# Key blocks of the first grouped attention in pairs on TensorE: two transposes, two gate pieces, two products

## What is computed

```python
def nsa_attention(...):            # 8 heads in 2 groups; per chunk of 128 queries
    sc = q @ kc * scale                       # 31 compressed keys
    ss = q @ k_slc * scale + bias             # selected keys (causal here)
    sw = q @ k_win * scale + bias             # window of 512 keys
    return gs[0] * softmax(sc) @ vc + gs[1] * softmax(ss) @ v_slc + gs[2] * softmax(sw) @ v_win
def swa_sink_attention(...):       # 8 heads, 2 kv heads, window of 128 keys, a sink in the softmax
    ...
y = sigmoid(gate_a) * (o_a @ w_up_nsa) + sigmoid(gate_b) * (o_b @ w_up_swa)
```

## Time and profile before

| | us |
|---|---|
| median of 3 runs | 1619.71 (1619.16 to 1621.48) |
| profiled execution | 1620.14 |
| its span in the trace | 1618.3 |
| the first grouped attention in it | about 130 to 332 |

### The profile page before, as it was taken

One profiled execution on the slowest core, in us unless ns is written; L12 is line 12 of the kernel. 1 busy time (PEld: TensorE's weight loads), 2 busy tenths in 40 slices (PEclk: granted clock), 3 DMA queues, 4 the chain that ended last, 5 costly groups with the idle time before them and its releaser, 6 DMA issues.

```text
span 1618.3 us, 23738 instructions
## 1 busy us (share of the span) xinstructions
PE 1553.6 (96%) x8400; PEld 1220.1 (75%) x8400; DVE 1002.4 (62%) x2286; ACT 757.2 (47%) x1426; POOL 504.8 (31%) x231
## 2 busy tenths in 40 slices
PE   7998999999899999999999999999999989999998
PEld 5886666678688888888887787778777768866666
DVE  6235546355679867655788756676677267147854
ACT  6225676634343323233444554445545443247753
POOL 3651232245244444444321212211114453320012
PEclk9999999999999999999999999999999989999998
DMA  6861112274356565653210111111101122220001
GB/s 200 174 165 34 60 59 67 72 271 131 104 175 202 184 201 189 197 152 92 79 53 27 40 40 39 40 51 33 44 26 57 49 67 91 66 67 13 1 23 57
DMA packets 48403, 149.35 MB, mean 92 GB/s; under 512 B 5783, under 2 KB 9111, under 8 KB 48185
## 3 DMA queue, kind: packets, MB, share of 16 engines
q1 hardware_dynamic: 37080, 112.45, 23.0%
q10 hardware_dynamic: 11232, 35.72, 6.8%
HBM read 141.53 MB, written 6.62 MB: 92 GB/s over the span
## 4 chain that ended last, share of the span: by engine, by line
PE 78%; DVE 8%; issue 5%; ACT 5%; POOL 1%; DMA 1%; ACTq 0%; POOLq 0%; DVEq 0%; SPq 0%
PE ps L357 40%; PE ps L361 19%; PE ps L583 4%; PE ps L594 3%; PE ps L564 3%; PE ps L1377 3%; PE ps L1336 2%; PE ps L1348 1%; POOL w_l L986 1%; PE ps L425 1%; PE ps L1091 1%; ACT w_h L340 1%; ACT sb L649 1%; DVE tg L1972 1%; DVE b_sb L688 1%
## 5 line engine op out<-in xcount | busy, mean ns | idle before, releaser
L986 POOL TENSOR_TENSOR w_l<-raw,w_h 128x1024 fp32r<-128x1024 f32 (+1 forms) x190 | 457.2, 2408 | 889.7 <-ACT w_h L340 869.5
L340 ACT ACTIVATE w_h<-raw 128x1024 fp32r<-128x1024 f32 x190 | 200.5, 1057 | 351.7 <-PE ps L357 293.0
L357 PE MATMUL ps<-x1h,w_h 128*128 128x512 f32 x584 | 237.9, 407 | 16.0 <-POOL w_l L986 10.4
L357 PE MATMUL ps<-x2h,w_h 128*128 128x512 f32 (+2 forms) x784 | 233.5, 361 | 13.6 <-DVE x2l L2045 4.8
L357 PE MATMUL ps<-x1h,w_l 128*128 128x512 f32 x584 | 230.7, 395 | 0.0
L361 PE MATMUL ps<-x1l,w_h 128*128 128x512 f32 x584 | 230.2, 394 | 0.0
L361 PE MATMUL ps<-x2l,w_h 128*128 128x512 f32 (+2 forms) x784 | 221.0, 345 | 0.0
L357 PE MATMUL ps<-x2h,w_l 128*128 128x512 f32 (+2 forms) x784 | 220.7, 345 | 0.0
L357 PEld LDWEIGHTS ps<-x2h,w_h 128*128 128x128 f32 x784 | 126.4, 189 | 42.3 <-issue 13.8
L357 PEld LDWEIGHTS ps<-x1h,w_h 128*128 128x128 f32 x584 | 111.5, 191 | 40.4 <-POOL w_l L986 10.9
L357 PEld LDWEIGHTS ps<-x2h,w_l 128*128 128x128 f32 x784 | 126.6, 189 | 19.5
(11 more groups left out here) (344 smaller groups left out, 2715.3 us busy)
## 6 DMA issues: line engine op xcount, KB each, us to landing
raw<-in_w_mlp SPq DMA_DIRECT2D x64, 512.0 KB, 3.7
mraw<-in_w_mod ACTq DMA_DIRECT2D x51, 512.0 KB, 3.7
raw<-in_w_a SPq DMA_DIRECT2D x32, 512.0 KB, 3.6
raw<-in_w_att SPq DMA_DIRECT2D x25, 512.0 KB, 11.5
raw<-in_w_b SPq DMA_DIRECT2D x20, 512.0 KB, 3.6
raw<-in_w_g SPq DMA_DIRECT2D x16, 512.0 KB, 3.6
raw<-in_w_ao SPq DMA_DIRECT2D x9, 512.0 KB, 3.6
gates<-g_stage ACTq DMA_DIRECT2D x16, 256.0 KB, 2.1
```

What stands on the lines that cost most here:

```text
L340: nc.scalar.activation(split(u)[0], raw[:, u % RAW], ACT.Copy).then_inc(w_hi, 1)
L357: mm = nc.tensor.matmul(o, w[:, k], xh(k), start=(first and k == k0 and wi == 0), stop=(last and k == k1 - 1 and wi == 1))
L986: nc.gpsimd.tensor_tensor(l[:, ks], raw[:, u % RAW, ks], h[:, ks].bitcast(F32), ALU.subtract).then_inc(w_lo, 1)
```

## The change

```diff
@@ -598,6 +598,15 @@
                     mm.then_inc(A.o, 1)
                 else:
                     mm.then_inc(A.k, 1)
+            if A.slots == 4 and nb > 1:
+                for b in range(0, nb, 2):
+                    for y in range(b, min(b + 2, nb)):
+                        turn(y)
+                    for y in range(b, min(b + 2, nb)):
+                        A.between_pe(pe, A.blk[n] + y)
+                    for y in range(b, min(b + 2, nb)):
+                        weigh(y)
+                return
             for b in range(nb):
                 turn(b)
                 A.between_pe(pe, A.blk[n] + b)
```

## The result

| | kernel before | changed kernel |
|---|---|---|
| median, us | 1619.43 (1617.43 to 1621.48, 6 runs) | 1651.19 (1646.99 to 1653.78, 6 runs) |
| profiled execution, us | 1620.14 | 1651.79 |
| its span, us | 1618.3 | 1650.0 |

The ratio is 1.0195, with a 95% interval of 1.0185 to 1.0206: the changed kernel is slower by 2%, 31.8 us. The forecast was 1650 us.

The account below looks back on a forecast made before the run. The prediction took TensorE to bound the first grouped attention, with any loss there arriving at the end. Its terms, 18.7 + 4.5 + 2.2 + 4.8 = +30.2 us, on a median of 1619.71 gave 1650 us, range 1638 to 1659 us.

Parts of the forecast that it names:

- The bare wait: Between a pair's transposes: the second waits 0.93 us for ScalarE's copy; with saved changes of work, 18.7 us over all steps.
- Late copies: Paired steps where ScalarE starts the copy late: the lateness, no longer hidden by a gate piece, adds 4.5 us.
- the three steps: Steps just behind a gate unit's end, where TensorE already waits for the copy: 0.55 us more each, 1.6 us.
- The six small ones: Six other steps whose first copy starts late with nobody waiting before: 2.0 us together, now showing in full.
- The product that waits longer: Two places where a lone block with a unit's end follows a pair: ScalarE's chain has 0.43 us less beside it, 0.9 us.
- One sign of the prediction: Paired steps in the profile after: waits of products for ScalarE's copy (L634) nearly gone.
- The gate's bank: Three pairs where a gate unit ends between adjacent gate pieces: the next piece waits for bank 5's copy, 2.2 us.
- The clock: TensorE's clock falls anew at the three steps of late copies, 1.6 us each: 4.8 us, bounds 0 to 12.8.
- the clock holds: Rival on TensorE's clock in the paired steps: no new falls, the lower bound of 0 us; chance 0.22.
- ScalarE is on time: Rival: ScalarE and VectorE get ahead, late copies mostly vanish, about 1640 us; chance 0.13.
- The clock falls often: Rival: eight falls or more in the paired steps, low clock bringing new waits, 1658 us or above; chance 0.17.
- Not slower: Rival: no wait between a pair's transposes, only saved changes between kinds of work, -3 us, 1617 us; chance 0.03.

Follow-up runs that it names:

- e9: Changed kernel plus matmuls with zeros into the gate's bank between the two transposes of each pair: 1643.88 us, ratio to the kernel before 1.0153.
- e1: Kernel before with only the products with the values grouped by twos, each transpose keeping its gate piece behind it: 1620.13 us, ratio 1.0000.
- e4: Changed kernel with half a gate piece (three matmuls) between the two transposes of a pair: 1631.84 us, ratio to the kernel before 1.0073.
- e10: Changed kernel, ScalarE copying half of each block's transposes an additional time before the whole copy: 1665.78 us.
- e7: Changed kernel, first block's copy made after two of the next step's four exponentials in steps right behind a gate unit's end: 1647.39 us.
- e2: Changed kernel with a pair's gate pieces apart again: both transposes, then piece, product, piece, product: 1661.77 us, 2.6% over the kernel before.
- e12: Kernel before with ScalarE's rounding of the next gate unit's weights moved behind the next block's copy: 1624.69 us, ratio 1.0031.
- e5: Changed kernel with ScalarE's copy out of bank 4 made by two instructions of 256 columns instead of one of 512: 1655.48 us.

## Why the prediction was right

*What bounds the stretch.* TensorE. The first matmul with the attention's output (o1h) started at 334.91 us before and starts at 367.76 us now: 32.9 us later. The spans differ by 31.7 us. The 1.2 us between them came in later stages, whose code is the same. The clock was a little higher there in this execution (from 1400 us on 0.97 before, in the same part now 0.98), which fits, but no run singles it out.

Of the 32.9 us, 0.9 us came in the very first step, which has one block and is untouched by the change: 5.79 us to the next step's transposes instead of 4.83, for most of it at half clock in both (granted clock 0.51 from 132 to 139 us before and from 134 to 141 us now). The same step takes 4.69 us in e9 and 5.52 us in e1, so this is a difference between executions. The paired steps bring the other 32.0 us. I read them from the start of one step's transposes to the start of the next step's.

*The bare wait, 18.7 us.* Right, in the size of each piece: 18.5 us. The transposes of a plain pair are 1.34 us apart, as worked out; a step of two blocks takes 5.71 us for 5.72; the time from step to step grew by 0.89 to 0.90 us in plain steps of two or three blocks (0.90 worked out) and by 1.48 in the plain step of four (1.52). e4 shows that cover removes it, e10 that it follows the copy's length, e1 that grouping the products does not cost.

*Late copies, 4.5 us.* Nearly right: about 4.1 us. The waits at the three steps are 2.58, 2.13 and 3.00 us where 1.19, 0.75 and 1.61 stood: 1.4 us more each, where 1.47 was worked out. That is some 0.46 us each over a plain pair, for 0.55. The six small ones are in full view too (1.14 us at the pair in which the earlier trace rows had 0.47 of lateness; 0.69 is the plain value) and make 2.3 us over the plain value. The product that waits longer because the one in front of it is already done is there as well, at one of the two places: 0.71 us instead of 0.29. At the other the time shows as lateness of the next copy, in the six. e7 showed the limit of this term: taking the lateness away moves it to VectorE. One sign of the prediction told nothing: the waits of products for the copy were to be nearly gone in paired steps, but all four stood in steps of one block before as now.

*The gate's bank, 2.2 us.* Right: three waits of 0.78 us where there was one of 0.34; e2 took 1.7 us of them away by putting products between.

*The clock, 4.8 us.* The term that was too small: about 7.2 us. The four steps in which the clock fell and had not fallen before grew by 2.71, 2.94, 2.68 and 4.65 us. The same steps of e9, where work in the waits kept the clock up, grew by 1.34, 1.36, 1.09 and 1.94 us; the differences are 1.4, 1.6, 1.6 and 2.7 us. That closes the sum: 18.5 + 4.1 + 2.2 + 7.2 = 32.0 us. The falls came at all three steps that I named, and at one more (246 to 251 us, behind scores of 32 columns, a wait of 0.38 us for VectorE and one of 0.87 us for the copy, with a granted clock of 0.50 from 248 to 250 us); the longest, from 287 to 295 us, lasted twice as long as the one in the earlier trace rows. The forecast took three falls of one length, 1.6 us each, the price of the one in the earlier trace rows (granted clock 0.50); it was the number and the length that were off. How many there are differs from run to run: the shortest run of the changed kernel, 1646.99 us, had a mean clock of 0.987, the longest, 1653.78 us, one of 0.981. The forecast took the fall of the earlier trace rows for the only one of the kernel before, but in that kernel the granted clock was 0.51 from 132 to 139 us as well; there are no pairs there, and no term of the sum hangs on it.

That the 31.8 us came within 2 us of 30.2 is mostly due to terms that each came out nearly right. Part is luck: the 0.9 us of the first step and the 1.2 us of the later stages, neither in the forecast, nearly cancel, and the clock was 2.4 us more than forecast.

*The rivals.* That the clock holds, to which the prediction gave 0.22, did not come true: the granted clock fell to 0.50 behind waits of 3.00, 2.58 and 2.13 us, behind one of 0.87 us, and in the earlier trace rows behind 0.64 us, while waits of 1.19 and 1.61 us in the kernel before had left it at 1.00. e9 shows that work in these waits keeps the clock up (0.98 in the stretch instead of 0.94). "ScalarE is on time" failed as argued: lateness that hangs on a gate unit's end was as long as before. "The clock falls often" had the right sign for this term, but its eight falls or more were not there; it counted on waits and scores of 32 columns, which stand ahead of the fall in the earlier trace rows. "Not slower" needed a hidden copy, which e1 and e4 show is what the old order provides.

## What to carry to other kernels

Before putting two users of one buffer next to each other, add up the time from the first one's start to the buffer's release, as the timeline shows it, and compare it with what stands between them: here 1.29 us of transposes and copy stood against 1.88 us of cover, and the move cut the cover to 0.41 us. Where the engine that now waits is the bound, the price is the part left open, 0.93 us, times the pairs, and here over a quarter more for a clock that fell in the waits (0.94 in the stretch instead of 0.97). When work is moved on an engine with time to spare, look at who starts because of it: an earlier copy and a later rounding both shortened the wait they were meant to shorten and brought longer ones elsewhere, by as much or more in the kernel before.

## What the runs showed of the hardware

Work with zeros in the waits made the kernel faster: 1643.88 us instead of 1651.19, with the stretch's granted clock at 0.98 instead of 0.94.

Beside a GpSimd subtraction of 2.35 us, four of VectorE's scalings took 3.30 us, against 1.14 us without it, 2.16 us more (e12). One of the four made up most of that: it started at 179.70 us and took 2.51 us, and the subtraction ran from 179.72 to 182.07 us. I had taken GpSimd, busy for 28% of the stretch, as out of the way.

Two ScalarE copies of 256 columns from PSUM without a wait between them take 0.66 us together, one of 512 columns 0.60 us: each lasts 0.38 us, but they start 0.28 us apart (e5).
